# A memory stage in unsplit fp32 with buffers of its own, and GpSimd's low parts in two instructions of 512 columns

## What is computed

```python
def first_block(x, mem, ...):
    h = rms_norm(x, norm_w)
    gq, gk, gv, glr, hq, hf, hi, xq, gate = split(h @ w_in)      # w_in: 1024 x 6160
    ...                                    # two gated linear attentions, 4 heads each
    m = rms_norm(mem, mem_norm_w)          # mem: 256 x 1024
    mk, mv = split(m @ w_mem_kv, 2)        # w_mem_kv: 1024 x 1024
    xo = softmax(xq @ mk.T * scale) @ mv   # per head
    mixed = concat(gla_o, hgrn_o, rms_norm(xo)) * silu(gate)
    x = x + mixed @ w_out
    return rms_norm(x, final_norm_w)

def second_block(x, ...):                  # 16 meta tokens ahead of x: 272 rows
    h = h + 0.5 * rmsnorm(swiglu(rmsnorm(h)))            # wi: 1024 x 5632, wo: 2816 x 1024
    h = h + rmsnorm(hybrid_mixer(rmsnorm(h)))            # 1024 x 7184, Fourier, short conv, delta rule
    h = h + 0.5 * rmsnorm(swiglu(rmsnorm(h)))
    return h[:, 16:]
```

## Time and profile before

| what | value |
|---|---|
| median of 3 runs | 1102.33 us (1102.14 to 1103.56) |
| the profiled execution's own time | 1100.94 us |
| its span, first to last instruction | 1099.1 us |
| mean granted TensorE clock | 0.968 |
| PE busy | 1025.7 us, 93% of the span |
| POOL busy | 726.6 us, 66% |
| DVE busy | 638.8 us, 58% |
| ACT busy | 478.0 us, 43% |
| moved by DMA | 154.89 MB, mean 141 GB/s |

### The profile page before, as it was taken

How to read it: one execution, slowest core, us unless ns; L and a number is a source line. 1 busy time by engine, 2 the same in 40 slices (tenths; PEclk the granted TensorE clock), 3 DMA queues, 4 the chain that set the end, 5 groups by cost and what they waited for, 6 DMA issues and landing times.

```text
span 1099.1 us, 21438 instructions
## 1 busy us (share of the span) xinstructions
PE 1025.7 (93%) x8206; PEld 1000.1 (91%) x8206; DVE 638.8 (58%) x1028; ACT 478.0 (43%) x706; POOL 726.6 (66%) x327
## 2 busy tenths in 40 slices
PE   4799999998989999998989999989999979999996
PEld 4699999998989999997888888989999969999995
DVE  6333995445855555345794653537556666656454
ACT  5344223445354444434546523433225455445431
POOL 3785655555848787996467723556538829889993
PEclk9899999999999999998999889989999989999998
DMA  7454334442636655565344213433335626555661
GB/s 260 134 175 152 116 116 117 134 134 76 193 104 185 179 166 183 162 191 151 112 138 135 59 40 95 135 97 119 100 91 145 208 70 190 180 184 183 180 194 55
DMA packets 47865, 154.89 MB, mean 141 GB/s; under 512 B 5980, under 2 KB 11108, under 8 KB 47604
## 3 DMA queue, kind: packets, MB, share of 16 engines
q1 hardware_dynamic: 45648, 151.31, 45.1%
q10 hardware_dynamic: 2152, 2.65, 0.7%
HBM read 151.85 MB, written 2.10 MB: 140 GB/s over the span
## 4 chain that ended last, share of the span: by engine, by line
PE 80%; DVE 9%; ACT 4%; issue 3%; POOL 3%; DMA 0%; DVEq 0%; SPq 0%; ACTq 0%; POOLq 0%
PE panel L1492 63%; PE panel L1536 4%; PE aux L1603 2%; POOL wlo L569 2%; PE aux L1791 1%; DVE qkv L1218 1%; DVE qkv L1222 1%; DVE qkv L1227 1%; PE aux L1521 1%; PE aux L1828 1%; PE aux L1867 1%; ACT whi L650 1%; PE aux L1876 1%; PE aux L1838 1%; PE aux L1544 1%
## 5 line engine op out<-in xcount | busy, mean ns | idle before, releaser
L569 POOL TENSOR_TENSOR wlo<-raw,whi 128x1024 fp32r<-128x1024 f32 x284 | 700.7, 2486 | 344.8 <-ACT whi L650 344.7
L1492 PE MATMUL panel<-xh,whi 128*128 128x256 f32 (+1 forms) x1504 | 442.5, 294 | 16.1 <-DVE xl L959 10.0
L1492 PE MATMUL panel<-xh,wlo 128*128 128x256 f32 (+1 forms) x1504 | 430.9, 287 | 0.0
L1492 PE MATMUL panel<-xl,whi 128*128 128x256 f32 (+1 forms) x1504 | 430.5, 286 | 0.0
L650 ACT ACTIVATE whi<-raw 128x1024 fp32r<-128x1024 f32 x284 | 294.2, 1052 | 188.1 <-PE panel L1492 153.6
L1492 PEld LDWEIGHTS panel<-xh,whi 128*128 128x128 f32 x1504 | 287.9, 191 | 20.7 <-issue 11.8
L1492 PEld LDWEIGHTS panel<-xl,whi 128*128 128x128 f32 x1504 | 286.9, 191 | 1.6
L1492 PEld LDWEIGHTS panel<-xh,wlo 128*128 128x128 f32 x1504 | 287.7, 191 | 0.0
L1492 PE MATMUL panel<-hh,whi 128*128 128x272 f32 (+1 forms) x352 | 100.1, 284 | 0.0
L1492 PE MATMUL panel<-hh,wlo 128*128 128x272 f32 (+1 forms) x352 | 99.9, 284 | 0.0
L1492 PE MATMUL panel<-hl,whi 128*128 128x272 f32 (+1 forms) x352 | 99.8, 284 | 0.0
(11 more groups left out here) (293 smaller groups left out, 1593.0 us busy)
## 6 DMA issues: line engine op xcount, KB each, us to landing
raw<-in_panels SPq DMA_DIRECT2D x236, 512.0 KB, 3.5
raw<-in_down SPq DMA_DIRECT2D x32, 448.0 KB, 3.3
raw<-in_down SPq DMA_DIRECT2D x16, 512.0 KB, 3.5
memx<-in_mem SPq DMA_DIRECT2D x1, 1024.0 KB, 5.1
h<-in_x SPq DMA_DIRECT2D x1, 1024.0 KB, 8.3
spill<-h ACTq DMA_DIRECT2D x1, 1024.0 KB, 4.7
h<-spill ACTq DMA_DIRECT2D x1, 1024.0 KB, 7.7
out<-h SPq DMA_DIRECT2D x2, 512.0 KB, 2.9
```

The lines of the kernel that those rows point to most:

```text
L569: nc.gpsimd.tensor_tensor(wlo[:, slot, :], raw[:, slot, :], whi[:, slot, :].bitcast(f32), ALU.subtract).then_inc(lo_ready, 1)
L1492: ins = M(bank[:, 0:w], wt[:, slot, P * t:P * t + P], x[:, kk, c0:c0 + w], start=first and m == 0 and n == 0, stop=last and m == len(pairs ...
```

## The change

Two parts.

**Memory stage.** Its 8 weight panels leave the ring: they are an array of their own (`mem_panels`), loaded once into four buffers (`memk`, `memk3`, `memv`) in space that `v`, `ot` and `gate` use later. They are not split. PE multiplies in fp32: 8 matmuls for an output instead of 24. `memg` (fp32, by ACT) takes the place of `memh` and `meml`. `mem` is loaded by four DMAs of 256 KB. The ring starts with the panels of `w_in`, four of which are loaded and split while PE does the memory stage. There are 276 ring panels now.

**Low parts.** `low` issues two instructions, of columns 0 to 511 and 512 to 1023, without a wait between them; the second raises `lo_ready`.

```diff
+MEMS = 8
+IN_P, WOUT_P, UP1_P = 0, 48, 64
...
-        memh = at("memh", ar, [P, KT, ROWS], f32r)
-        meml = at("meml", ar + 2048, [P, KT, ROWS], f32r)
+        memg = at("memg", ar, [P, KT, ROWS])
+        memk = at("memk", ar + 8192, [P, 3, 1024])
+        memk3 = at("memk3", ar + 21504, [P, 1024])
+        memv = at("memv", ar + 17408, [P, 4, 1024])
...
             sp.dma_start(vec[:, 0:VECS], a["vec"]).then_inc(vec_in, 16)
-            sp.dma_start(memx[:], a["mem"]).then_inc(mem_in, 16)
-            sp.dma_start(raw[:, 0, :], a["panels"][0]).then_inc(raw_ready[0], 16)
+            sp.dma_start(memx[:, 0:2, :], a["mem"][:, 0:2, :]).then_inc(mem_in[0], 16)
+            sp.dma_start(mem_panel(0), a["mem_panels"][0]).then_inc(mem_weights[0], 16)
+            for j in range(1, 4):
+                sp.dma_start(memx[:, 2 * j:2 * j + 2, :], a["mem"][:, 2 * j:2 * j + 2, :]).then_inc(mem_in[j], 16)
+            sp.dma_start(mem_panel(1), a["mem_panels"][1]).then_inc(mem_weights[1], 16)
             sp.dma_start(ones[:], a["ones"]).then_inc(ones_in, 16)
             sp.dma_start(h[:, :, META:LEN], a["x"]).then_inc(x_in, 16)
-            for r in range(1, RING):
+            sp.dma_start(mem_panel(2), a["mem_panels"][2]).then_inc(mem_weights[2], 16)
+            for r in range(RING):
                 sp.dma_start(raw[:, r, :], a["panels"][r]).then_inc(raw_ready[r], 16)
+                sp.dma_start(mem_panel(3 + r), a["mem_panels"][3 + r]).then_inc(mem_weights[3 + r], 16)
+            sp.dma_start(mem_panel(7), a["mem_panels"][7]).then_inc(mem_weights[7], 16)
...
-                nc.gpsimd.tensor_tensor(wlo[:, slot, :], raw[:, slot, :], whi[:, slot, :].bitcast(f32),
-                                        ALU.subtract).then_inc(lo_ready, 1)
+                for half in (slice(0, 512), slice(512, 1024)):
+                    ins = nc.gpsimd.tensor_tensor(wlo[:, slot, half], raw[:, slot, half], whi[:, slot, half].bitcast(f32),
+                                                  ALU.subtract)
+                ins.then_inc(lo_ready, 1)
...
-            for o in range(8):
-                ahead(MEM_P + o)
-
-            pool.wait_ge(split_low, 8)
+            ahead(IN_P)
+
+            pool.wait_ge(squared, 8)
             nc.gpsimd.memset(s[:], 0.0).then_inc(s_zero, 1)
...
-            act.wait_ge(mem_in, 16)
             for kk in range(KT):
-                A(memh[:, kk, :], memx[:, kk, :], ACT.Identity, scale=vcol("mem_norm", kk)).then_inc(split_high, 1)
-            high(16, None, 0)
-            nxt[0] = 1
+                if kk % 2 == 0:
+                    act.wait_ge(mem_in[kk // 2], 16)
+                A(memg[:, kk, :], memx[:, kk, :], ACT.Identity, scale=vcol("mem_norm", kk)).then_inc(mem_gained, 1)
             squares(0)
-            ahead(MEM_P + 1 - LEAD)
             act.wait_ge(x_in, 16)
             squares(1)
+            ahead(IN_P - LEAD + 1)
             act.wait_ge(eps_set, 1)
             pre_root(0)
-            ahead(MEM_P)
             act.wait_ge(rstd_ready, 1)
             post_root(1)
+            ahead(IN_P - LEAD + 2)
             for kk in range(KT):
                 act.wait_ge(scaled, kk + 1)
                 A(xh[:, kk, 0:ROWS], tmp[:, kk, 0:ROWS], ACT.Copy).then_inc(split_high, 1)
-                if kk == 3:
-                    ahead(MEM_P + 1)
-            for o in range(2, 8):
-                ahead(MEM_P + o)
+            ahead(IN_P)
...
-            for kk in range(KT):
-                low_part(0, kk, "mem_norm", 0)
             add_squares(0)
...
+                for kk in range(KT):
+                    if i == 0:
+                        pe.wait_ge(mem_gained, kk + 1)
+                    ins = M(pb[o % 4][:, 0:ROWS], mem_panel(i)[:, P * kk:P * kk + P], memg[:, kk, :],
+                            start=kk == 0, stop=kk == KT - 1)
+                ins.then_inc(passed, 1)
...
+                    for kk in range(KT):
+                        ins = M(pb[o % 4][:, 0:2 * P], memg[:, kk, P * rt:P * rt + P],
+                                memv[:, i - 4:i - 2, P * kk:P * kk + P], start=kk == 0, stop=kk == KT - 1)
+                    ins.then_inc(passed, 1)
```

More of the change, by code:

```diff
@@ L19 @@
 FLOOR = 1e-30
-MEM_P, IN_P, WOUT_P, UP1_P = 0, 8, 56, 72
+MEMS = 8
+IN_P, WOUT_P, UP1_P = 0, 48, 64
 DOWN1_P = UP1_P + UP
@@ L185, in passes @@
     out, panel, n = {}, {}, 0
-    for i in range(56):
+    for i in range(MEMS):
         n += 1
-        out[MEM_O + i] = panel[MEM_P + i] = n
+        out[MEM_O + i] = n
+    for i in range(48):
+        n += 1
+        out[IN_O + i] = panel[IN_P + i] = n
     for k, (i, _) in enumerate(W_OUT):
@@ L386, in build @@
         more_in = sem("more_in")
-        mem_in = sem("mem_in")
+        mem_in = [sem(f"mem_in{i}") for i in range(4)]
         x_in = sem("x_in")
@@ L463, in build @@
         raw_ready = [sem(f"raw_ready{i}") for i in range(RING)]
+        mem_weights = [sem(f"mem_weights{i}") for i in range(MEMS)]
+        mem_gained = sem("mem_gained")
         bank_free = [sem(f"bank_free{i}") for i in range(4)]
@@ L501, in build, with mem_panel @@
         W = [ROWS, ROWS, ROWS, LEN, LEN, LEN, ROWS, ROWS, ROWS]
-        SPLIT = {0: 0, 1: 1, 3: 2, 5: 3, 7: 4}
+        SQUARES = {0: 0, 1: 1, 3: 2, 5: 3, 7: 4}
+        SPLIT = {1: 0, 3: 1, 5: 2, 7: 3}
+        def mem_panel(i):
+            return memk[:, i, :] if i < 3 else memk3[:] if i == 3 else memv[:, i - 4, :]
         def hcol(w):
@@ L955, in low_part @@
             def low_part(n, kk, name, at0):
-                src, hi_, lo_ = (memx, memh, meml) if n == 0 else (h[:, :, hcol(W[n])], xh, xl)
+                src, hi_, lo_ = h[:, :, hcol(W[n])], xh, xl
                 dve.wait_ge(split_high, 8 * SPLIT[n] + kk + 1)
@@ L983, in add_squares @@
                 for kk in range(1, KT):
-                    dve.wait_ge(squared, 8 * SPLIT[n] + kk + 1)
+                    dve.wait_ge(squared, 8 * SQUARES[n] + kk + 1)
                     ins = TT(y[:, 0, 0:W[n]], y[:, 0, 0:W[n]], y[:, kk, 0:W[n]], ALU.add)
@@ L1043, in _ @@
             for kk in range(KT):
-                dve.wait_ge(split_high, 8 + kk + 1)
+                dve.wait_ge(split_high, 8 * SPLIT[1] + kk + 1)
                 TT(xl[:, kk, 0:ROWS], tmp[:, kk, 0:ROWS], xh[:, kk, 0:ROWS].bitcast(f32), ALU.subtract).then_inc(split_low, 1)
@@ L1519, in first_output @@
                     ins = products(pb[o % 4], p % RING, [(kk, kk)], xh, xl, 0, w, kk == 0, kk == KT - 1)
-                    pe.wait_ge(squared, 8 * SPLIT[n] + kk + 1)
+                    pe.wait_ge(squared, 8 * SQUARES[n] + kk + 1)
                     total = M(bank[:, 0:w], ones[:], sq[:, kk, 0:w], start=kk == 0, stop=kk == KT - 1)
@@ L1555, in w_out, with mem_output, mem_rows @@
                          half == 0, half == 1).then_inc(passed, 1)
[L1558 to L1565, removed]
+            def mem_output(i):
+                o = MEM_O + i
+                pe.wait_ge(mem_weights[i], 16)
+                if o >= 4:
+                    pe.wait_ge(bank_free[o % 4], o // 4)
+                for kk in range(KT):
[4 more added lines that the diff above has]
+                ins.then_inc(passed, 1)
+            def mem_rows(i):
+                for n in range(2):
+                    pe.wait_ge(mem_weights[i + n], 16)
+                for rt in range(2):
+                    o = MEM_O + i + rt
+                    pe.wait_ge(bank_free[o % 4], o // 4)
+                    for kk in range(KT):
+                        ins = M(pb[o % 4][:, 0:2 * P], memg[:, kk, P * rt:P * rt + P],
+                                memv[:, i - 4:i - 2, P * kk:P * kk + P], start=kk == 0, stop=kk == KT - 1)
+                    ins.then_inc(passed, 1)
+            for i in range(4):
+                mem_output(i)
+                if i == 0:
+                    pe.wait_ge(ones_in, 16)
+                if i < 2:
+                    norm_stat(i)
+            mem_rows(4)
+            mem_rows(6)
             pe.wait_ge(more_in, 11 * 16)
-            pe.wait_ge(split_low, 16)
+            pe.wait_ge(split_low, 8)
             for step in FIRST:
@@ L1996 @@
     w_out = np.stack([w_out[i, :, half] for i, half in W_OUT])
-    panels = np.concatenate([pack(x["w_mem_kv"], KT)] + [pack(p, KT) for p in (hf, gk, gq, hq, xq, gate, gv, hi)]
+    panels = np.concatenate([pack(p, KT) for p in (hf, gk, gq, hq, xq, gate, gv, hi)]
                             + [w_out, up(x["ffn1_wi_2"]), np.stack(mixer), pack(x["w_out_2"], KT), up(x["ffn2_wi_2"])])
@@ L2011 @@
              "dt_bias": np.broadcast_to(x["dn_dt_bias_2"].reshape(1, 8), (P, 8))}
-    arrays = {"panels": panels, "down": down, "x": rows(x["x"]), "mem": rows(x["mem"]), "meta": rows(x["meta_tokens_2"]),
+    arrays = {"panels": panels, "mem_panels": pack(x["w_mem_kv"], KT), "down": down, "x": rows(x["x"]), "mem": rows(x["mem"]), "meta": rows(x["meta_tokens_2"]),
               "vec": np.concatenate([table[n] for n in VEC_AT], 1), "upw": x["gla_w_gate_up"],
```

## The result

| | before | changed |
|---|---|---|
| median of the runs | 1102.74 us | 1089.91 us |
| lowest and highest, 6 runs each | 1101.52 to 1103.56 | 1087.78 to 1094.11 |
| ratio, with its 95% interval | | 0.9895 (0.9876 to 0.9913) |
| profiled execution | 1100.94 | 1091.45 |
| its span | 1099.1 | 1089.7 |

The change is faster by 1.05%: 11.6 us by the ratio, 12.8 by the medians, where 19.4 were forecast. The time lies inside the range, at its upper end, and outside the forecast's own 1079 to 1086. The changed kernel's times scatter more than before's: three at 1087.8 to 1088.4, three at 1091.5 to 1094.1.

What follows compares the result with a forecast made beforehand. PE bound the kernel, busy 93% of the span. Memory stage -12.4 and low parts in two -7.0 made -19.4 us: 1100.94 to 1081.5 profiled, 1082.9 as median; own range 1079 to 1086, 8 in 10 1074 to 1091.

Steps and rivals of the forecast that it cites:

- Memory stage, -12.4: At the start: the first panel of `w_in` comes at 41.8 us instead of 54.19, saving 12.4 us.
- The wait at the sum of squares: Memory stage, after output 0: PE waits 1.2 us for the squares by ACT and their adding by DVE.
- thin cover: Memory stage: bank 0 free near 20, needed at 24.4; bank 2 near 29, needed at 31.3; otherwise 1 to 2 lost.
- POOL's cost of halves: Low parts: a half takes 1.26 us, a panel 2.52 instead of 2.33; about 0.5 us on the path in all.
- The halves, -7.0: Low parts in two: blocked DVE instructions wait for less, -7.5 us, and with POOL's 0.5 cost -7.0.
- 10.3 priced before the discount: Sum of the gains priced at PE's single waits for DVE, 10.3 us, of which two thirds were taken.
- the convolution (-4.0 and -1.0): Mixer's convolution: -4.0 us from the 4.6 without a matmul at 571 to 603 us, -1.0 from L1238's wait.
- the norm after the mixer (-2.0): At L1007, where DVE is more than 2 us behind: -2.0 of PE's 3.0 us wait.
- L1118 (-0.9): At the decay step: -0.9 of PE's 1.9 us wait.
- L1166 (-1.0): A DVE instruction 2.77 us long that PE waits for: -1.0 us.
- a little clock: Part of the rival that DVE's waits shrink fully: shorter idling leaves PE's half level out; 1077.5 us, chance 0.17.
- the port is not handed over between the halves: Rival: DVE gets in only at the second half's end, so only POOL's 0.5 to 2 us remain; 1091, chance 0.15.

Runs made afterwards that it cites:

- filler: Changed kernel plus three fp32 products, results overwritten, ahead of PE's wait for the gather: 1085.69 us; the same on the memory stage alone, without halves: 1091.54 us.
- quarters: Changed kernel with each low part in four instructions of 256 columns instead of two of 512: 1115.35 us, ratio 1.0143.
- selected halves: Memory stage alone, plus halves only for panels made in the mixer's first steps and its output panels: 1085.11 us, ratio 0.9845.

## Why the prediction was right or wrong

- **Memory stage, -12.4: right in mechanism, nearly in size.** 11.1 us at 43 us, and alone 10.7 there and 10.2 at the last panel. The product's 0.432 us, not the 0.475 by the four-pass rule of the Trainium skill (FP8 and Floating Point Precision, TensorE Precision Notes), decided, as argued. The missing 1.3 us: `memg` was done at 9.75 us instead of near 8.6, the squares behind it came 1.1 us late, and the sums took 1.0 instead of 0.8. PE started at 6.36 instead of 5.7, but that isn't on the path. The wait at the sum of squares was there, 1.1 us. Neither thin cover failed: PE waits for no bank before 43 us. DVE's scaled tiles were blocked by halves, as feared, and bank 2 was still free in time.
- **POOL's cost of halves: right.** 1.26 us each, a panel 2.52 at least; PE waits 0.8 us for POOL in two places, less than the 3.7 with wholes.
- **The halves, -7.0: wrong.** Alone they measured 0.24%, 2.6 us, and on top of the memory stage nothing beyond the intervals. The gains that were priced came in. The step that failed is the cost: "the cost on the path is only where PE waits for a low part at all, about 0.5 us in all". In the column of halves alone the steps down add up to 11.5 us, against 10.3 priced before the discount, and the steps up to 7.7, against 0.5. Most of the steps up begin at DVE: instructions that stand in a run and weren't blocked before are now blocked by the next half, or by the next panel's. The forecast priced each DVE instruction by itself ("waits for the rest of 1.2 us, not of 2.4") and asked only of those that were blocked already. The trace before had the sign: two in a row at 2.63 and 2.62, one per POOL instruction. (Two thirds of 10.3 are 6.9, not 7.5; the slip doesn't change the verdict.)
- **The places.** Of those priced, the convolution (-4.0 and -1.0) and the norm after the mixer (-2.0) came in: -4.4 and -2.8. L1118 (-0.9) came in with -2.5 at the first level, with an avoided half pace, and L1166 (-1.0) with -1.4 between 247 and 280 us of halves alone, but the changed kernel gained nothing there. Not priced at all were the decay levels (+3.5) and the stretch from 640 to 866 (+3.7), where the tiles ahead of the output panels stand: 1.3 us more of waits for `xl` with halves alone, most of the rest PE's half pace behind them.
- **PE's half pace.** The forecast left it out but for "a little clock". From 620 to 645 us of before's time the changed kernel's two profiles lose 4.0 and 2.4 us. That the halves cause it isn't shown: halves alone and the kernel without halves in the levels have them in the convolution too and lose 0.1 us or less there. The filler helps in one profile with halves and not in one without. What sorts one execution into the cluster at 1088 and another into that above 1091 stays open.
- **The rivals.** That the port is not handed over between the halves is refuted as a rule: in the levels and the convolution DVE starts after each half. But it isn't always handed over, as 2.67 us with halves and 30.03 with quarters show. By number this rival, 1091, came nearest, for a reason that it did not give: luck, not mechanism.

## What to carry to other kernels

Cutting a long instruction on a shared port shortens each block and adds blocks. In a run of DVE instructions each added piece lets one more pass, which is worth that one's own short time and can be less than what the earlier phases of the engines cost. It pays where few instructions are blocked in a row and something unblockable stands between them, and only where PE waits for the result, directly or through ACT. Here it freed 80 us of DVE and 2.6 us of the kernel. Don't cut so finely that the pieces never pause: one DVE instruction stood still for 30 us. And when a stage leaves an engine idle, price the pace of what follows as well.

## What was not expected

- A DVE stream that is under way can keep the port: before, eight tiles ran through and POOL's instruction took 3.21 us instead of 2.40. It doesn't always: in the changed kernel a half started at 851.18 with the third tile still running, took 1.29 us, and the fourth tile, at 851.25, took 1.50. Pieces change who gets there first, so the same cut moved the stall from POOL, where it cost nothing, to DVE, where PE waited.
- One DVE instruction was held 30.03 us by quarters that each take 0.7.
- 1.3 us of discarded products at one place of a 1090 us kernel went with 2.8 to 3.4 us in the profile (-11.1 and -10.5 to -13.9 at 645 us).
- The changed kernel's times scatter over 6 us or more, before's over 4, and the selected halves' over 2.3.
